# A second feed-forward block in 6, 8 and 8 chunks, with high parts cast by ScalarE

## The reference, cut to what matters

```
h = rmsnorm(x, norm_ffn_pre)
f = (silu(h @ ffn_w_gate) * (h @ ffn_w_up)) @ ffn_w_down      # 1024 -> 2816 -> 1024
x = x + rmsnorm(f, norm_ffn_post)
```

## Time and profile before

| | us |
|---|---|
| median of 3 runs | 1759.29 (1759.22 to 1760.31) |
| the profiled execution | 1759.92 |
| its span | 1758.1 |
| PE busy | 1735.3 (99%) |
| POOL busy | 1165.9 (66%) |
| DVE busy | 897.3 (51%) |
| ACT busy | 597.4 (34%) |

### The profile page before, as it was taken

One profiled execution on the slowest core, in us unless ns is written; L12 is line 12 of the kernel. 1 busy time (PEld: TensorE's weight loads), 2 busy tenths in 40 slices (PEclk: granted clock), 3 DMA queues, 4 the chain that ended last, 5 costly groups with the idle time before them and its releaser, 6 DMA issues.

```text
span 1758.1 us, 25603 instructions
## 1 busy us (share of the span) xinstructions
PE 1735.3 (99%) x9543; PEld 1451.0 (83%) x9543; DVE 897.3 (51%) x1583; ACT 597.4 (34%) x1196; POOL 1165.9 (66%) x1241
## 2 busy tenths in 40 slices
PE   7999999999999999999999999999999999999998
PEld 5786768899899887878888888777888888998997
DVE  6447666764165254262005373555433569773753
ACT  3236663355065122222014232554300222450542
POOL 6643558957657786666766665554778599677574
PEclk9999999999999999999999999999999999999999
DMA  6620012323323232223332222212233222324231
GB/s 220 211 75 28 25 49 101 105 96 109 108 82 110 98 114 90 83 72 100 100 100 71 75 73 86 66 68 73 73 99 106 84 90 88 111 86 132 75 115 64
DMA packets 48075, 163.10 MB, mean 93 GB/s; under 512 B 5614, under 2 KB 8750, under 8 KB 47696
## 3 DMA queue, kind: packets, MB, share of 16 engines
q1 hardware_dynamic: 46744, 158.28, 27.1%
q10 hardware_dynamic: 1208, 3.18, 0.6%
HBM read 158.41 MB, written 2.11 MB: 91 GB/s over the span
## 4 chain that ended last, share of the span: by engine, by line
PE 93%; DVE 2%; POOL 1%; ACT 1%; issue 1%; DMA 1%; ACTq 0%; SPq 0%; DVEq 0%; POOLq 0%
PE bank L980 92%; POOL w_lo_t L3066 1%; PE bank L1384 1%; PE bank L1430 1%; DMA x_sb<-in_x 0%; POOL w_hi_t L3061 0%; DMA kv_raw<-att_l_t 0%; DVE sq_sum L2176 0%; ACT h_hi L1879 0%; ACT sq L1645 0%; DVE x_sb L2625 0%; DVE sig L2305 0%; DVE cmp_xt L2615 0%; ACT att_pt L2022 0%; DVE h_lo L2424 0%
## 5 line engine op out<-in xcount | busy, mean ns | idle before, releaser
L3066 POOL TENSOR_TENSOR w_lo_t<-w_raw,w_hi_t 128x256 fp32r<-128x256 f32 (+1 forms) x809 | 690.1, 883 | 18.1
L3061 POOL TENSOR_SCALAR w_hi_t<-w_raw 128x1024 fp32r<-128x1024 f32 (+1 forms) x217 | 243.9, 1124 | 386.3 <-PE bank L980 351.6
L980 PE MATMUL bank<-h_hi,w_hi_t 128*128 128x512 f32 (+1 forms) x1192 | 434.9, 365 | 9.1 <-ACT h_hi L1879 8.3
L980 PE MATMUL bank<-h_hi,w_lo_t 128*128 128x512 f32 (+1 forms) x1192 | 423.7, 356 | 0.0
L980 PE MATMUL bank<-h_lo,w_hi_t 128*128 128x512 f32 (+1 forms) x1192 | 420.1, 355 | 0.4 <-DVE h_lo L2424 0.3
L980 PEld LDWEIGHTS bank<-h_hi,w_hi_t 128*128 128x128 f32 x1192 | 226.3, 190 | 51.6 <-issue 19.2
L980 PEld LDWEIGHTS bank<-h_lo,w_hi_t 128*128 128x128 f32 x1192 | 225.4, 189 | 34.1 <-issue 1.7
L980 PEld LDWEIGHTS bank<-h_hi,w_lo_t 128*128 128x128 f32 x1192 | 226.4, 190 | 31.1 <-issue 1.2
L980 PE MATMUL bank<-hid_hi,w_hi_t 128*128 128x512 f32 (+1 forms) x439 | 170.4, 388 | 1.7 <-DVE hid_lo L2309 0.9
L980 PE MATMUL bank<-hid_lo,w_hi_t 128*128 128x512 f32 (+1 forms) x439 | 169.6, 386 | 0.0
L980 PE MATMUL bank<-hid_hi,w_lo_t 128*128 128x512 f32 (+1 forms) x439 | 169.6, 386 | 0.0
(11 more groups left out here) (424 smaller groups left out, 3121.8 us busy)
## 6 DMA issues: line engine op xcount, KB each, us to landing
w_raw<-in_w SPq DMA_DIRECT2D x261, 512.0 KB, 3.4
w_more<-in_w SPq DMA_DIRECT2D x15, 512.0 KB, 3.6
y<-in_w SPq DMA_DIRECT2D x6, 512.0 KB, 5.3
x_sb<-in_x SPq DMA_DIRECT2D x4, 512.0 KB, 7.4
x_sb<-in_x ACTq DMA_DIRECT2D x1, 1536.0 KB, 6.7
u_raw<-in_w SPq DMA_DIRECT2D x2, 512.0 KB, 5.4
toep<-table SPq DMA_DIRECT2D x4, 256.0 KB
decay<-in_decay SPq DMA_DIRECT2D x1, 1024.0 KB, 4.8
```

The lines of the kernel that those rows point to most:

```text
L980: return pe.matmul(out, lhs, rhs, start=start, stop=stop, **kw)
L3061: pool.tensor_scalar(hi[:, 0:cols], src[:, 0:cols], 1.0, 0.0, ALU.mult, ALU.add).then_inc(*did("w_hi", i))
L3066: ins = pool.tensor_tensor(lo[:, piece], src[:, piece], hi.bitcast(F32)[:, piece], ALU.subtract)
```

## The change

`PARTS2` becomes (6, 8, 8): the first group has one plain chunk less, the last one pair more. Four more things change with it:

- ACT, not POOL, makes the high parts of the slots from `fg` of chunk 4 to `fu` of chunk 5 (`ACT_HI`). Each cast stands in ACT's program at the step at which the slot it replaces was last used, ahead of ACT's own share of that step.
- The slots of the first `down2` group leave `IN_PIECES`: their low parts are made in one operation of 1024 columns.
- The high part of each plain hidden chunk is a copy by ACT instead of a cast by DVE, and DVE makes the low part one step later, behind the next chunk's gate product.
- The last pair of each pair group is finished in its banks: the gate's sigmoid and the products are written to banks c and d, high parts are copied and low parts subtracted from there, half by half, by ACT and DVE.

```diff
-PARTS2 = (7, 8, 7)
+PARTS2 = (6, 8, 8)
-IN_PIECES = range(SLOTS["cqr"][0], SLOTS[("pair2", 1, 0)][0])
+IN_PIECES = range(SLOTS["cqr"][0], SLOTS[("down2", 0)][0])
+ACT_HI = range(SLOTS[("fg", 0, 4)][0], SLOTS[("down2", 0)][0])
+HI_AT = {}
+for i in ACT_HI:
+    HI_AT.setdefault(LAST_USE[BEHIND[i]], []).append(i)
...
 # ScalarE
+        def last_gate(name):
+            act.wait_ge(*after("prod_d2", name, "gate"))
+            act.activation(pair_half(name, "c"), gate_rows(name)[0][:, RIGHT], ACT.Sigmoid).then_inc(*did("sg", name, 1))
+            for b, side in (("c", RIGHT), ("d", LEFT)):
+                act.wait_ge(*after("prod_d2", name, b))
+                act.activation(hid2[0][:, name[2], side], pair_half(name, b), ACT.Copy).then_inc(*did("hid_s2", name, b))
...
-        for step in ORDER:
+        for at, step in enumerate(ORDER):
             stage = step[0]
+            for i in HI_AT.get(at, ()):
+                act.wait_ge(*landed(i))
+                act.wait_ge(*slot_done[BEHIND[i]])
+                act.activation(w_hi[RING[i]], raw(i), ACT.Copy).then_inc(*did("wa_hi", i))
...
+                elif key == "fu":
+                    n = name[2]
+                    act.wait_ge(*evacuated(name))
+                    act.activation(hid2[0][:, n], tmp[:, n % 2], ACT.Copy).then_inc(*did("hid_s2", "fu", n))
 # VectorE
+        def plain_low(n):
+            own("hid_s2", "fu", n)
+            dve.tensor_tensor(hid2[1][:, n], tmp[:, n % 2], hid2[0][:, n].bitcast(F32), ALU.subtract)\
+               .then_inc(*did("hid", "down2", 0, n))
...
             g, s, u = gate_rows(last)
-            dve.wait_ge(*evacuated((last, "c")))
+            own("prod_d2", last, "gate")
             chain(dve.tensor_tensor(u[:, RIGHT], u[:, RIGHT], g[:, RIGHT], ALU.mult))
             own("sg", last, 1)
-            dve.tensor_tensor(u[:, RIGHT], u[:, RIGHT], s[:, RIGHT], ALU.mult).then_inc(*did("prod_d2", last, 0))
-            pair_c21(last)
+            dve.tensor_tensor(pair_bank(last, "c"), u[:, RIGHT], pair_bank(last, "c"), ALU.mult).then_inc(*did("prod_d2", last, "c"))
+            own("st_pe", last, Q_W22)
+            chain(dve.tensor_tensor(pair_bank(last, "d"), u2_t, pair_bank(last, "d"), ALU.add))
             dve.wait_ge(*evacuated((last, "a")))
-            dve.tensor_tensor(u[:, LEFT], u[:, LEFT], g[:, LEFT], ALU.mult).then_inc(*did("prod_d2", last, 1))
-            own("prod_d2", last, 0)
-            own("prod_d2", last, 1)
-            own("hid_s2", last)
-            dve.tensor_tensor(hid2[1][:, last[2]], u, hid2[0][:, last[2]].bitcast(F32), ALU.subtract)\
-               .then_inc(*did("hid_d2", last))
+            dve.tensor_tensor(pair_bank(last, "d"), g[:, LEFT], pair_bank(last, "d"), ALU.mult).then_inc(*did("prod_d2", last, "d"))
+            for b, side in (("c", RIGHT), ("d", LEFT)):
+                own("prod_d2", last, b)
+                own("hid_s2", last, b)
+                hi, lo = [h[:, last[2], side] for h in hid2]
+                dve.tensor_tensor(lo, pair_bank(last, b), hi.bitcast(F32), ALU.subtract).then_inc(*release((last, b)))
...
             if stage == "st_norm":
                 key = step[1]
+                if key == "fpre":
+                    plain_low(PARTS2[0] - 1)
...
                     dve.tensor_tensor(sig2[:, n % 2], ps(name)[:], r_h[:], ALU.mult).then_inc(*release(name))
                     dve.wait_ge(*evacuated(name))
+                    if n:
+                        plain_low(n - 1)
...
-                    dve.tensor_tensor(t, ps(name)[:], s, ALU.mult).then_inc(*release(name))
-                    dve.wait_ge(*evacuated(name))
-                    split(t, hid2[0][:, n], hid2[1][:, n], "hid", "down2", 0, n)
+                    if n >= 2:
+                        own("hid", "down2", 0, n - 2)
+                    dve.tensor_tensor(tmp[:, n % 2], ps(name)[:], s, ALU.mult).then_inc(*release(name))
 # GpSimd
-            pool.tensor_scalar(hi[:, 0:cols], src[:, 0:cols], 1.0, 0.0, ALU.mult, ALU.add).then_inc(*did("w_hi", i))
-            pool.wait_ge(*after("w_hi", i))
+            if i in ACT_HI:
+                pool.wait_ge(*after("wa_hi", i))
+            else:
+                pool.tensor_scalar(hi[:, 0:cols], src[:, 0:cols], 1.0, 0.0, ALU.mult, ALU.add).then_inc(*did("w_hi", i))
+                pool.wait_ge(*after("w_hi", i))
```

More of the change, by code:

```diff
@@ L444 @@
 SEMAPHORES = """x_in0 x_in1 x_in2 x_in3 x_back ones_set r_cols mask_in mixer_in kv_in ksw_in kr_in kr_turn kr_again mla_w zeros table_out const_in wqb_in misc_in late_in alibi_in alibi_s bias_in y_out
-w_hi w_lo slot_used v_chain s_chain sq_s sq_v rstd rstd_used
+w_hi wa_hi w_lo slot_used v_chain s_chain sq_s sq_v rstd rstd_used
 h_t h_hi hy_hi u_hi h_ready bcast_v gate_v nsa_v sq_hi sq_lo cmpx cmp_s cmp_v att_l att_n att_exp att_p att_tr att_done
@@ L448 @@
 o_ready o_hi m_ready gla_v gla_s gla_kd gla_st gla_a gla_done gla_t prod gate_s merged merged_hl q_s swa_neg swa_m swa_n swa_s swa_p swa_done ft lo_t table last_t last_x last_sum last_f last_r last_c last_l last_y first_hi first_lo
-st_h st_t st_xhi st_xlo st_s st_hi st_lo st_pe st_u2 st_q st_c22 hid_p hid_d st_r wq_hi sg prod2 prod_d2 g_right hid_s2 hid_p2 hid_d2""".split()
+st_h st_t st_xhi st_xlo st_s st_hi st_lo st_pe st_u2 st_q st_c22 hid_p hid_d st_r wq_hi sg prod2 prod_d2 g_right hid_s2 hid_p2""".split()
 class Counts:
@@ L745, in pair_low, with pair_half @@
         return after("hid_d" if by_vector(n, c) else "hid_p", n, c)
+    def pair_half(name, b):
+        return ps((name, b))[:, 0:T // 2]
     def last_left(c):
@@ L750, in gate_low @@
     def gate_low(name):
-        return after("hid_d2" if name[2] == PARTS2[name[1]] - 1 else "hid_p2", name)
+        return evacuated((name, "d")) if name[2] == PARTS2[name[1]] - 1 else after("hid_p2", name)
     def gate_free(eng, name):
@@ L1773, in gate_right, with gate_high @@
             act.activation(s[:, RIGHT], g[:, RIGHT], ACT.Sigmoid).then_inc(*did("sg", name, 1))
-        def gate_high(name, product):
-            act.activation(hid2[0][:, name[2]], product, ACT.Copy).then_inc(*did("hid_s2", name))
+        def gate_high(name):
+            act.wait_ge(*after("prod2", name))
+            act.activation(hid2[0][:, name[2]], gate_rows(name)[0], ACT.Copy).then_inc(*did("hid_s2", name))
+        def last_gate(name):
[4 more added lines that the diff above has]
+                act.activation(hid2[0][:, name[2], side], pair_half(name, b), ACT.Copy).then_inc(*did("hid_s2", name, b))
         def pair_phase(pairs):
@@ L1805, in pair_phase @@
                 else:
-                    act.wait_ge(*after("prod2", old))
-                    gate_high(old, gate_rows(old)[0])
+                    gate_high(old)
             last = pairs[-1]
@@ L1814, in pair_phase @@
                 gate_left(last)
[L1815 to L1818, removed]
-        for step in ORDER:
+                last_gate(last)
+        for at, step in enumerate(ORDER):
             stage = step[0]
+            for i in HI_AT.get(at, ()):
+                act.wait_ge(*landed(i))
+                act.wait_ge(*slot_done[BEHIND[i]])
+                act.activation(w_hi[RING[i]], raw(i), ACT.Copy).then_inc(*did("wa_hi", i))
             if stage == "st_norm":
@@ L2250, in pair_c22, with pair_c12 @@
             dve.tensor_tensor(to, q_t, pair_bank(name, "d"), ALU.add).then_inc(*did("st_c22", name))
-        def pair_c12(name):
+        def pair_c12(name, last=False):
             if name[0] == "pair":
@@ L2261, in pair_c12 @@
             dve.wait_ge(*after("st_pe", name, Q_S4))
-            dve.tensor_tensor(to, u2_t, pair_bank(name, "c"), ALU.add).then_inc(*release((name, "c")))
+            dve.tensor_tensor(to, u2_t, pair_bank(name, "c"), ALU.add)\
+               .then_inc(*did("prod_d2", name, "gate") if last else release((name, "c")))
         def pair_c21(name):
@@ L2291, in pair_phase @@
             pair_c22(last)
-            pair_c12(last)
+            pair_c12(last, not up)
             if up:
@@ L2560, in _ @@
                     dve.wait_ge(*full(name))
-                    t = tmp[:, n % 2]
-                    dve.tensor_tensor(t, ps(name)[:], s, ALU.mult).then_inc(*release(name))
-                    dve.wait_ge(*evacuated(name))
-                    split(t, hid2[0][:, n], hid2[1][:, n], "hid", "down2", 0, n)
+                    if n >= 2:
+                        own("hid", "down2", 0, n - 2)
+                    dve.tensor_tensor(tmp[:, n % 2], ps(name)[:], s, ALU.mult).then_inc(*release(name))
             elif stage == "tm" and step[4] < step[5] - 1:
```

## The result

The changed kernel takes 1769.2 us (median of 4, 1768.59 to 1770.33) against 1759.26 for the one before (1758.97 to 1760.31): ratio 1.0056, 95% interval 1.0041 to 1.0072, clear of no change. The profiled execution has a span of 1767.7 with a mean granted clock of 0.996, before 1758.1 and 0.998. It is slower by 9.9; I had forecast 7.2.

A forecast was written before the change was run, and what follows sets the result against it. PE, busy 99% of the span, was taken as the bound. -3.36 + 3.5 + 7.05 = +7.2 on the profiled 1759.92 gave 1767.1, or 1766.5 from the runs' median; range 1761.0 to 1769.5.

The forecast's parts named there:

- Work and old waits: One plain chunk exchanged for a pair, net -0.76, and three waits in the down2 groups gone (-1.15, -0.30, -1.15): -3.36 us.
- The last product's ending: Behind PE's last product, add, product, ACT's copy and low part take some 2.1 us; PE needs it 4.76 later.
- ACT's late cast: Plain part, fu of chunk 4: cast behind chunks 0 to 2 in ACT's order makes PE wait, +3.5 us.
- DVE's input sums: First down2 group, output 6: PE waits for DVE's third copy; 7.05 us waited in the whole group.
- The hidden low part: Chunk 5's low part on DVE waits for POOL, ends 4.41 after E (last plain chunk's end); PE waits 1.1.
- the big operations: DVE's 11 operations of 1024 columns take turns with POOL; the last ends 29.5 us after the last plain chunk.
- the clock: PE's clock at the new waits: the forecast sum counted no loss from a fall.
- the clock's rival: Both new waits, and the clock halves for 3.4 us in the 5.7 wait at output 6: +1.7, 1768.2; chance 0.15.

The follow-up runs named there:

- e1: The changed kernel, but POOL makes the high parts of the four slots again (ACT_HI empty): 1765.68 us against 1759.51 for the kernel before, 1.0034.
- e9: The changed kernel with only ACT's cast of fu 4 moved forward, ahead of its sigmoid of chunk 1: 1765.27 us against 1759.96 before, 1.0032.
- e5: The changed kernel, but POOL splits only 8 of 1024 columns of slots 3 to 5 of the first down2 group: 1761.36 us, 1.0011.
- e2: The changed kernel with the first down2 group's low parts in pieces of 256 columns again: 1767.07 us against 1759.51 before, 1.0044.
- e3: The kernel before the change with parts 6, 8, 8 alone: 1767.20 us against 1759.51, 1.0044.
- e4: The changed kernel with parts 7, 8, 7: 1768.39 us against 1759.51 for the kernel before, 1.0050.

## Why the prediction was right

The places, the engines that hold PE there and the order of events came as forecast. The sizes:

- **Work and old waits** (-3.36): a pair takes 10.08 (16 in 161.3), the waits of before are gone. From the first matmul of chunk 3 to the end of the span the changed kernel takes 341.2 and the one before 331.5; less the terms below that leaves -3.4. The last product's ending was forecast at 2.1 behind PE; it was:

```profile
1710.80 0.42 DVE L2336 TENSOR_TENSOR hid_lo<-bank,hid_hi 128x256 fp32r<-128x256 f32 x1
1711.41 0.42 DVE L2336 TENSOR_TENSOR hid_lo<-bank,hid_hi 128x256 fp32r<-128x256 f32 x1 [0.19 <-ACT hid_hi L1791]
```

  It ends at 1711.83, 2.0 behind 1709.80.
- **ACT's late cast** (+3.5): 3.0 with restart. The chain came as forecast; the cast ended at 1441.87 against 1442.35, mostly because chunks 1 and 2 took DVE 3.51 each where I had 3.65. e1 and e9 show the cause from two sides.
- **DVE's input sums** (+7.05): 6.85. The hidden low part ended at E + 4.41 (forecast 4.41), the big operations at E + 29.3 (29.5), PE went on at E + 31.4 (31.5). e5 shows the cause; e2 shows that the one-go form adds 2.3 of it.
- **The failed term is the clock.** The sum had it at nothing, and a rival had it at +1.7 for one wait, with 0.15. It fell at both waits: 3.2. Less the 0.7 by which the two terms above were too large, that is 2.5 of the 2.7 between 9.9 and 7.2. My argument against it was that the fall at 229.70 in the trace of before came without a long standstill. The runs show that it is no rare chance: at waits of 4.2 to 5.5 it fell in all six profiles that have one (the changed kernel, e1, e2, e3, e4, e9), for 3.4 or 6.8 us; behind waits of 2.7 to 3.0 in three of five (there, e2, e4; not e3, e5). What decides between the three and the two, no run here shows. The fall near 229 us isn't tied to the change: e2, e3 and e9 lack it, the eight other profiles have it. Stretches that come or stay away like this may be why the times of these kernels spread over 2 to 3 us; that is not shown, since each has one profile.

So the time came inside the range by some luck. What happened is the clock's rival twice over, which I had not listed, and 1769.2 is 0.3 under the range's upper end. It is inside only by the 1.3 that I had set aside for a longer wait.

The Trainium skill's rule for the port shared by DVE and POOL (SBUF — State Buffer, Who interferes with whom) agrees with these rows: 3.30 for a sum that takes 1.22 alone, and 1.22 again in e5, where POOL has next to nothing to do. On the clock, the Trainium skill (TensorE: Matmul & The Clock Gate, HAM oscillation) warns of idle gaps of PE. The six falls at waits of 4.2 to 5.5 agree; the three at waits of about 2.7 say to count shorter ones too than those it warns of.

## What to carry to other kernels

Work given to an idle engine must be placed where that engine's own queue has got to, not where the data is free: one line moved is worth about 4 us here, of which 1.6 is the clock's. Before the work that covers a side chain is shortened, measure that chain with its slack (0.8 us here) and count the other engine's operations that hold it up; one long operation frees that engine and blocks its neighbour (e2). A wait of PE costs more than itself once the clock follows it.

## What was unexpected of the hardware

Standstills of PE of about 2.7 us went with 3.4 us at half clock in three profiles of four (e5 is the fourth), and those of 4.9 to 5.5 with 6.8 us in three of four. In e3 PE multiplied through most of such a stretch, at half clock:

```profile
1491.35:1498.18 6.83, 6.22 (x15) 4.86 (x16) 6.04 (x10) 1.72 (x4) 0.00 (x0) 0.50 0.28 77
```

That adds 1.6 to about 3 us to a wait of 5: 1.6 in the changed kernel, 2.0 in e9, 2.8 in e1, 3.1 in e3.
